# Transposing the normed x tiles by DMA, SBUF to SBUF, in place of TensorE transposes

## The chip, the cores and the metric

The kernel runs on the 8 cores of one Trainium2 chip. Each core computes 2048 of the 16384 tokens, with no traffic between cores. The metric is the device time of the slowest core in microseconds (us).

## The reference

One decoder block on x of shape (2, 8192, 2048), float32. Two gated token mixers share one input projection:

```python
h = rmsnorm(x, norm1_g[l])
proj = h @ w_in[l]                    # (B, T, 15872)
# mixer A: dilated windows (128,1), (512,4), (2048,16), 3 groups of 8 heads, merged by denominators
# mixer B: window 128, 16 query heads over 2 kv heads, with sinks
merged = gate_a * (o_a @ w_branch_a[l]) + gate_b * (o_b @ w_branch_b[l])
x = x + merged @ w_out[l]
h2 = rmsnorm(x, norm2_g[l])
x = x + jnp.square(jax.nn.relu(h2 @ w_ff1[l])) @ w_ff2[l]
```

## The kernel before

A core holds its own 2048 tokens and the 2048 before them (the halo, needed by the window of 2048): 4096 rows of x, loaded as 32 tiles of 128 rows x 2048 columns float32. The first stage norms each tile and turns it round, so that the 2048 features lie on the partitions, in 16 chunks of 128: hH holds the halo, hO the own tokens, both as [128, 16, 2048] bf16. The rest of the kernel multiplies weights with these two: keys and values of mixer A and B, then queries with the attention, the gates, the output projection and the MLP.

The instructions of each engine are written out in order by helpers (P.op, P.group, P.dma); each carries the waits that its buffers ask for. Five queues run side by side: PE, ACT, DVE, POOL (loads weights) and SP (all other DMAs of this stage). An instruction that waits holds up all behind it on its own queue.

The stage that the change touches is a loop over j = 0 to 31 that begins each turn with norm_tile(j + 2) and transpose_tile(j + 1), and then multiplies: va_job(1, j - 4) from j = 4 on and va_job(0, j) always. A va_job is 16 matmuls of tile j against 512 columns of w_in (L395), an eviction by ACT (L403) or DVE (L406) to vst, and a store of 128 KB by SP (L413). After the loop four va_jobs of slab 1 are left, then the key heads of the 2048 window start (L494).

norm_tile(j) does, on ACT, the sum of squares of the loaded tile xt (L363, its elementwise result is thrown away into xs), then a logarithm and an exponential (L365, L367) for the scale; on DVE the multiplication by scale and gain into xs (L369), bf16; then SP is asked for the load of tile j + 3 (xload, L351), 1 MB. There are three xt and two xs. transpose_tile(j) does 16 TensorE transposes in two groups of 8 into PSUM banks 4 to 7 (L380), which ACT (L388) and DVE (L390) copy to hH or hO, 1024 elements a partition each.

The whole order of a turn:

```python
    for j in range(32):
        if j + 2 < 32:
            norm_tile(j + 2)
        if j + 1 < 32:
            transpose_tile(j + 1)
        if j >= LEAD:
            va_job(1, j - LEAD)
        va_job(0, j)
```

From the 41st va_job on, tick() has POOL copy a piece of the MLP weights to DRAM as bf16 at every fourth job (w1c, L323).

Of the kernel before, what the change touches and what calls it, by code (L numbers as in the profile page):

```python
# [11 lines left out]
BF16 = mybir.dt.bfloat16  # L12
AF = mybir.ActivationFunctionType
# [4 lines left out]
TOWN = 2048  # L18
# [224 lines left out]
def build_program():  # L243
    nc = bass.Bass("TRN2", target_bir_lowering=False)

    def dram(name, shape, dt, kind):
        return nc.dram_tensor(name, list(shape), dt, kind=kind).ap()
# [14 lines left out]
    out = dram("out", [NCH, 128, TOWN], F32, "ExternalOutput")  # L262
# [10 lines left out]
    P = Prog(nc)  # L273
    psum = [nc.alloc_psum_tensor(f"bank{i}", [128, 512], F32) for i in range(8)]
    bank = [Buf(f"bank{i}") for i in range(8)]
# [3 lines left out]
    ident = carea.at("ident", [128, 128], BF16, 0)  # L279
# [6 lines left out]
    st = [carea.at(f"st{i}", [128, 4], F32, 768 + 32 * i) for i in range(3)]  # L286
# [10 lines left out]
    B_const = Buf("consts")  # L297
# [30 lines left out]
    hO = A.at("hO", [128, NCH, TOWN], BF16, OWN)  # L328
    hH = A.at("hH", [128, NCH, TOWN], BF16, HAL)
    B_h = [Buf(f"h{j}") for j in range(32)]  # L330
# [9 lines left out]
    xt = [A.at(f"xt{i}", [128, D], F32, RX + 8192 * i) for i in range(3)]  # L340
    B_xt = [Buf(f"xt{i}") for i in range(3)]
    xs = [A.at(f"xs{i}", [128, D], BF16, RX + 24576 + 4096 * i) for i in range(2)]
    B_xs = [Buf(f"xs{i}") for i in range(2)]
    B_st = [Buf(f"st{i}") for i in range(3)]
    vst = [A.at(f"vst{i}", [128, 512], BF16, VST + 1024 * i) for i in range(4)]
    B_vst = [Buf(f"vst{i}") for i in range(4)]
    B_vn = {g: Buf("vn_" + g) for g in vn}
# [2 lines left out]
    def xload(j):  # L350
        P.dma("sp", lambda e: e.dma_start(out=xt[j % 3][:], in_=xe[128 * j:128 * j + 128, :]), B_xt[j % 3],  # L351
              writes=[B_xt[j % 3]])
# [7 lines left out]

    def norm_tile(j):
        s, x3, t3 = j % 2, j % 3, j % 3
        P.op("act", lambda e: e.activation(out=xs[s][:], in_=xt[x3][:], func=AF.Square, accum_out=st[t3][:, 0:1]),  # L363
             reads=[B_xt[x3]], writes=[B_xs[s], B_st[t3]])
        P.op("act", lambda e: e.activation(out=st[t3][:, 1:2], in_=st[t3][:, 0:1], func=AF.Ln, scale=1.0 / D,  # L365
                                           bias=EPS), writes=[B_st[t3]])
        P.op("act", lambda e: e.activation(out=st[t3][:, 2:3], in_=st[t3][:, 1:2], func=AF.Exp, scale=-0.5),  # L367
             writes=[B_st[t3]])
        P.op("dve", lambda e: e.scalar_tensor_tensor(out=xs[s][:], in0=xt[x3][:], scalar=st[t3][:, 2:3], in1=g1b[:],  # L369
                                                     op0=ALU.mult, op1=ALU.mult),  # L370
             reads=[B_xt[x3], B_st[t3], B_g1b], writes=[B_xs[s]])
        if j + 3 < 32:
            xload(j + 3)

    def transpose_tile(j):
        s = j % 2
        for half in range(2):
            bi = 4 + (2 * j + half) % 4
            pb = psum[bi][:].bitcast(BF16)
            fns = [(lambda e, c=8 * half + k, k=k, pb=pb, s=s: e.transpose(  # L380
                out=pb[:, 128 * k:128 * k + 128], in_=xs[s][:, 128 * c:128 * c + 128], identity=ident[:]))
                for k in range(8)]
            P.group("pe", fns, reads=[B_xs[s], B_const], writes=[bank[bi]])
            h, t0 = (hH, 128 * j) if j < 16 else (hO, 128 * j - TOWN)
            dst = h[:, 8 * half:8 * half + 8, t0:t0 + 128]
            src = pb.rearrange("p (a b) -> p a b", a=8)
            if half == 0:
                P.op("act", lambda e, dst=dst, src=src: e.copy(out=dst, in_=src), reads=[bank[bi]], adds=[B_h[j]])  # L388
            else:
                P.op("dve", lambda e, dst=dst, src=src: e.tensor_copy(out=dst, in_=src), reads=[bank[bi]],  # L390
                     adds=[B_h[j]])

    def v_block(lhs, bufs, wps, kper, ncols, g, blk, col0, bi):

# [40 lines left out]

    LEAD = 4
    norm_tile(0)
    P.dma("sp", lambda e: e.dma_start(out=gvec[:], in_=gvec_in[:, :]), cb2, writes=[cb2])
    P.dma("sp", lambda e: e.dma_start(out=esink[:], in_=sinks_in.partition_broadcast(128)), cb3, writes=[cb3])
    P.dma("sp", lambda e: e.dma_start(out=g2[:], in_=g2_in[:, :]), cb4, writes=[cb4])  # L440
    P.dma("sp", lambda e: e.dma_start(out=rtab[:], in_=rtab_in[:, :, :]), B_rtab, writes=[B_rtab])
    norm_tile(1)
    transpose_tile(0)
# [8 lines that stand above are left out]
# [33 lines left out]
    def main_bank():  # L485
        bi = mctr[0] % mode["main"]
        mctr[0] += 1
        return bi
# [336 lines left out]
    for st_ in range(STEPS):  # L825
        u, f = divmod(st_, 4)
# [29 lines left out]
    for i in range(24):  # L856
        P.dma("sp", lambda e, i=i: e.dma_start(out=oT[:, i, :], in_=oTd[i]), B_oT[i], reads=[B_oTd[i]],  # L857
              writes=[B_oT[i]])
# [33 lines left out]
    for i, (n, tb) in enumerate(its):  # L892
        if i + 2 < len(its):
# [5 lines left out]
        fns = [(lambda e, k=k, tsl=tsl, b1=b1, wa=wa: e.matmul(psum[b1][:, :], lhsT=wa[:, 128 * k:128 * k + 128],  # L899
                                                              rhs=oT[:, k, tsl], start=(k == 0), stop=(k == 7)))  # L900
               for k in range(8)]
        P.group("pe", fns, reads=[ba] + B_oT[:8], writes=[bank[b1]])
        fns = [(lambda e, k=k, tsl=tsl, b2=b2, wbt=wbt: e.matmul(  # L903
            psum[b2][:, :], lhsT=wbt[:, 128 * k:128 * k + 128], rhs=oT[:, 8 + k, tsl], start=(k == 0),
            stop=(k == 15))) for k in range(16)]
# [4 lines left out]
        s = 2 * (i % 3)  # L910
        for j, b in ((0, b1), (1, b2)):
# [4 lines left out]
             reads=[B_gt[s], B_gt[s + 1]], adds=[B_mT[n]])  # L916
# [45 lines left out]
    for i, (n, tb) in enumerate(its):  # L962
        wt, wb = ld.get(pc[0] + n)
        if i + NXT - 1 < len(its):
            xrload(i + NXT - 1)
        bi = main_bank()
        fns = [(lambda e, k=k, tb=tb, bi=bi, wt=wt: e.matmul(  # L967
            psum[bi][:, :], lhsT=wt[:, 128 * k:128 * k + 128], rhs=mT[:, k, 512 * tb:512 * tb + 512],
            start=(k == 0), stop=(k == NCH - 1))) for k in range(NCH)]
# [51 lines left out]
    for tb in range(4):  # L1021
        tsl = slice(512 * tb, 512 * tb + 512)
        for sl in range(16):
# [3 lines left out]
            for ci in range(4):  # L1027
                j = 4 * sl + ci
                bi = main_bank()
                fns = [(lambda e, k=k, ci=ci, bi=bi, wt=wt, tsl=tsl: e.matmul(  # L1030
                    psum[bi][:, :], lhsT=wt[:, 512 * k + 128 * ci:512 * k + 128 * ci + 128],
                    rhs=h2T[:, k, tsl], start=(k == 0), stop=(k == NCH - 1))) for k in range(NCH)]
# [4 lines left out]
                     reads=[bank[bi]], writes=[B_rt[rs_]])  # L1037
                P.op("dve", lambda e, bi=bi, rs_=rs_, j=j: e.scalar_tensor_tensor(  # L1038
                    out=uT[:, j, :], in0=psum[bi][:, :], scalar=0.0, in1=rt[rs_][:], op0=ALU.max, op1=ALU.mult),
                    reads=[bank[bi], B_rt[rs_]], writes=[B_u[j]])  # L1040
# [4 lines left out]
        for n in range(NCH):  # L1045
# [6 lines left out]
                  reads=[B_x2s], writes=[B_yr[ys]])  # L1052
            bi = main_bank()
            for j0 in range(0, 64, 16):
                fns = [(lambda e, j=j, bi=bi, wt=wt: e.matmul(  # L1055
                    psum[bi][:, :], lhsT=wt[:, 128 * j:128 * j + 128], rhs=uT[:, j, :],
                    start=(j == 0), stop=(j == 63))) for j in range(j0, j0 + 16)]
                P.group("pe", fns, reads=[wb] + B_u[j0:j0 + 16], writes=[bank[bi]])
            P.op("dve", lambda e, bi=bi, yos=yos, tsl=tsl: e.tensor_tensor(  # L1059
                out=yo[yos][:], in0=psum[bi][:, :], in1=r2b[:, tsl], op=ALU.mult),  # L1060
                reads=[bank[bi], B_r2[tb]], writes=[B_yo[yos]])
            P.op("dve", lambda e, yos=yos, ys=ys: e.tensor_tensor(out=yo[yos][:], in0=yo[yos][:], in1=yr[ys][:],
                                                                 op=ALU.add),
                 reads=[B_yr[ys]], writes=[B_yo[yos]])
            P.dma("sp", lambda e, yos=yos, n=n, tsl=tsl: e.dma_start(out=out[n, :, tsl], in_=yo[yos][:]), B_yo[yos],
                  reads=[B_yo[yos]])
# [114 lines left out]
```

How the kernel before makes its waits and increments, by code:

```python
    def replay(self, eng_name, eng):  # L141
        waited = {}
        for waits, fn, s, n in self.q[eng_name]:
            for ws, v in waits:
                if waited.get(ws.name, 0) < v:
                    eng.wait_ge(ws.h, v)
                    waited[ws.name] = v
            if fn is None:
                continue
            ins = fn(eng)
            if s is not None:
                ins.then_inc(s.h, n)
```

## Time and profile before

| | us |
|---|---|
| three runs | 4761.35, 4761.61, 5371.22; median 4761.61 |
| the profiled execution | 4764.82 |
| its slowest core, from first to last instruction (core 5) | 4763.3 |
| the other seven cores | 4723.3 to 4758.1 |
| PE busy | 4663.0 (98%) |
| first stage, up to the first key matmul (L494) | 296.5 |

The profile is of core 5. Its times count from the first instruction. A "busy" PE has matmuls under way; they are pipelined, so the mean of a single one (379 ns for 512 columns) is longer than what one adds to a stream (16 in 3.45 us). A releaser is what ended the idle time of an engine.

### The profile page before, as it was taken

The numbers are of one execution on the slowest core, as the hardware profiler recorded it, in microseconds if no ns is written. First come the engines' busy times: TensorE is split into PE (matmuls) and PEld (weight loads), VectorE is DVE, ScalarE is ACT, GpSimd is POOL, SyncE is SP. The second block draws the span as 40 slices with busy tenths as digits, with TensorE's granted clock in tenths as the row PEclk, the third lists the DMA queues.
The fourth block names the chain that finished last, engine by engine and source line by source line (L and its number), as shares of the span: only waits on it lengthen the run. The fifth ranks groups of instructions, "written<-read, shape, count | busy, mean of one in ns | idle before, by whom it ended". The sixth has DMA issues, their size and how long they took to land.

```text
span 4763.3 us, 64896 instructions; the slowest of 8 cores (4723.3 to 4763.3 us)
## 1 busy us (share of the span) xinstructions
PE 4663.0 (98%) x24018; PEld 2228.6 (47%) x24018; DVE 1607.2 (34%) x1806; ACT 1394.1 (29%) x2424; POOL 294.9 (6%) x560
## 2 busy tenths in 40 slices
PE   6999999988999999999999999999999999999999
PEld 3544445544455455555444444444444444444444
DVE  3446650112555555655424433210121111101111
ACT  4534430034455555555412233210011001001100
POOL 0000000000011111111110000000000000000000
PEclk9999999999999999999999999999999999999999
DMA  8685567775666556565486666435534544454354
GB/s 203 173 132 91 104 98 106 128 118 95 125 113 131 118 132 137 110 138 110 106 211 137 145 178 180 166 145 191 192 144 168 185 177 159 162 196 168 146 190 144
DMA packets 225766, 696.94 MB, mean 146 GB/s; under 512 B 96944, under 2 KB 109232, under 8 KB 200752
## 3 DMA queue, kind: packets, MB, share of 16 engines
q0 software_dynamic: 57536, 455.12, 39.8%
q1 hardware_dynamic: 167920, 237.67, 17.1%
q8 instruction: 197, 3.23, 0.3%
q14 instruction: 113, 0.93, 0.1%
HBM read 727.70 MB, written 185.20 MB: 192 GB/s over the span
## 4 chain that ended last, share of the span: by engine, by line
PE 94%; DMA 3%; ACT 1%; SPq 1%; issue 0%; DVE 0%; DVEq 0%; ACTq 0%
PE bank L494 22%; PE bank L1030 19%; PE bank L1055 19%; PE bank L395 10%; PE bank L804 7%; PE bank L967 5%; PE bank L903 5%; PE bank L899 2%; PE bank L749 1%; PE bank L509 1%; PE bank L700 1%; PE bank L754 1%; DMA oTd<-ost 1%; DMA xt<-xe 1%; SPq L857 1%; DMA vn_a<-vst 1%
## 5 line engine op out<-in xcount | busy, mean ns | idle before, releaser
L494 PE MATMUL bank<-hO,w 128*128 128x512 bf16 x3968 | 915.9, 381 | 12.8 <-DVE Qt L519 12.8
L1030 PE MATMUL bank<-h2T,ws 128*128 128x512 bf16 x4096 | 886.0, 379 | 2.1 <-ACT h2T L950 2.1
L1055 PE MATMUL bank<-uT,ws 128*128 128x512 bf16 x4096 | 884.7, 379 | 0.0
L1030 PEld LDWEIGHTS bank<-h2T,ws 128*128 128x128 bf16 x4096 | 401.1, 98 | 486.7 <-issue 4.7
L1055 PEld LDWEIGHTS bank<-uT,ws 128*128 128x128 bf16 x4096 | 400.8, 98 | 483.3
L494 PEld LDWEIGHTS bank<-hO,w 128*128 128x128 bf16 x3968 | 382.4, 98 | 446.2 <-issue 23.6
L1036 ACT ACTIVATE rt<-bank 128x512 f32<-128x512 f32 x256 | 152.8, 597 | 1394.2 <-PE bank L1030 1394.2
L804 PE MATMUL bank<-hO,w 128*128 128x512 bf16 x2048 | 476.6, 379 | 0.0
L1038 DVE SCALAR_TENSOR_TENSOR uT<-bank,rt 128x512 bf16<-128x512 f32 x256 | 177.1, 692 | 711.2 <-ACT rt L1036 711.2
L519 DVE SCALAR_TENSOR_TENSOR kst<-bank,gvec,rb 128x512 bf16<-128x512 f32 (+1 forms) x154 | 293.3, 1904 | 254.7 <-ACT rb L513 249.2
L395 PE MATMUL bank<-w,hO 128*128 128x512 bf16 (+1 forms) x1472 | 304.1, 363 | 10.7 <-DVE vst L406 10.7
L804 PEld LDWEIGHTS bank<-hO,w 128*128 128x128 bf16 x2048 | 200.3, 98 | 241.2
L1059 DVE TENSOR_TENSOR yo<-bank,r2b 128x512 f32<-128x512 f32 x64 | 44.3, 692 | 788.7 <-PE bank L1055 788.7
L502 ACT ACTIVATE sq<-bank 128x512 bf16<-128x512 f32 x314 | 183.9, 586 | 413.7 <-PE bank L494 413.7
L519 DVE SCALAR_TENSOR_TENSOR Qt<-bank,gvs,rb 128x512 bf16<-128x512 f32 x160 | 232.0, 1450 | 162.5 <-ACT rb L513 162.4
L511 ACT ACTIVATE rb<-bank 128x512 f32<-128x512 f32 x314 | 183.8, 585 | 251.3 <-PE bank L509 249.4
L903 PE MATMUL bank<-oT,w 128*128 128x512 bf16 x1024 | 233.3, 381 | 3.7 <-DMA oT<-oTd 3.7
L967 PE MATMUL bank<-mT,w 128*128 128x512 bf16 x1024 | 221.3, 379 | 0.1
L395 PEld LDWEIGHTS bank<-w,hO 128*128 128x128 bf16 x1472 | 150.6, 103 | 150.0 <-issue 10.9
L513 ACT ACTIVATE rb<-rb 128x512 f32<-128x512 f32 x314 | 194.5, 620 | 29.0 <-ACT rb L511 0.4
L704 ACT ACTIVATE Pexp<-bank 128x512 f32<-128x512 f32 x320 | 173.4, 596 | 54.7 <-PE bank L700 53.9
L406 DVE CAST vst<-bank 128x512 bf16<-128x512 f32 (+1 forms) x77 | 51.0, 664 | 407.5 <-PE bank L395 334.2
(100 smaller groups left out, 3443.9 us busy)
## 6 DMA issues: line engine op xcount, KB each, us to landing
ws<-w1c POOLq DMA_DIRECT2D x64, 2048.0 KB, 8.2
ws<-w2c POOLq DMA_DIRECT2D x64, 2048.0 KB, 8.9
w<-w_in POOLq DMA_DIRECT2D x115, 512.0 KB, 8.1
xt<-xe SPq DMA_DIRECT2D x32, 1024.0 KB, 6.3
w1c<-w_ff POOLq DMA_DIRECT2D x64, 512.0 KB, 7.5
w2c<-w_ff POOLq DMA_DIRECT2D x64, 512.0 KB, 7.1
gz<-zst POOLq DMA_DIRECT2D x128, 256.0 KB, 3.7
gt<-gz SPq DMA_DIRECT2D x128, 256.0 KB, 4.3
```

The source lines that it names most:

```text
L395: fns = [(lambda e, k=k: e.matmul(psum[bi][:, 0:ncols], lhsT=lhs[k], rhs=wps[k // kper][0][:, (k % kper) * ncols:(k % kper + 1) * ncols], ...
L494: fns = [(lambda e, k=k: e.matmul(psum[bi][:, 0:n], lhsT=wt[:, 128 * k:128 * k + 128], rhs=hB[:, k, :] if last else hsl(k, t0, n), start=( ...
L502: P.op("act", lambda e: e.activation(out=sq[es][:, 0:n], in_=psum[bi][:, 0:n], func=AF.Square), reads=[bank[bi]], writes=[B_sq[es]])
L511: P.op("act", lambda e: e.activation(out=rb[er][:, 0:n], in_=psum[b2][:, 0:n], func=AF.Ln, bias=128.0 * EPS), reads=[bank[b2]], writes=[B_ ...
L513: P.op("act", lambda e: e.activation(out=rb[er][:, 0:n], in_=rb[er][:, 0:n], func=AF.Exp, scale=-0.5), writes=[B_rb[er]])
L519: P.op("dve", lambda e: e.scalar_tensor_tensor(out=dst, in0=src, scalar=gsrc[:, gcol:gcol + 1], in1=r, op0=ALU.mult, op1=ALU.mult), reads= ...
L804: fns = [(lambda e, k=k: e.matmul(psum[bi][:, :], lhsT=wt[:, 128 * k:128 * k + 128], rhs=hO[:, k, 512 * tb:512 * tb + 512], start=(k == 0) ...
L903: fns = [(lambda e, k=k, tsl=tsl, b2=b2, wbt=wbt: e.matmul(psum[b2][:, :], lhsT=wbt[:, 128 * k:128 * k + 128], rhs=oT[:, 8 + k, tsl], star ...
L967: fns = [(lambda e, k=k, tb=tb, bi=bi, wt=wt: e.matmul(psum[bi][:, :], lhsT=wt[:, 128 * k:128 * k + 128], rhs=mT[:, k, 512 * tb:512 * tb + ...
L1030: fns = [(lambda e, k=k, ci=ci, bi=bi, wt=wt, tsl=tsl: e.matmul(psum[bi][:, :], lhsT=wt[:, 512 * k + 128 * ci:512 * k + 128 * ci + 128], r ...
L1038: P.op("dve", lambda e, bi=bi, rs_=rs_, j=j: e.scalar_tensor_tensor(out=uT[:, j, :], in0=psum[bi][:, :], scalar=0.0, in1=rt[rs_][:], op0=A ...
L1055: fns = [(lambda e, j=j, bi=bi, wt=wt: e.matmul(psum[bi][:, :], lhsT=wt[:, 128 * j:128 * j + 128], rhs=uT[:, j, :], start=(j == 0), stop=( ...
```

## The change

transpose_tile no longer uses TensorE. SP issues one DMA transpose for each tile, from xs straight into the tile's 128 columns of hH or hO. Each of the two xs has a semaphore of its own for it (B_tr). The 512 transposes on PE, the 32 copies on ACT and the 32 on DVE are gone. The sum of squares now throws its elementwise result into hH or hO, where the transpose overwrites it, no longer into xs.

```diff
--- before.py
+++ after.py
@@ -342,6 +342,7 @@
     xs = [A.at(f"xs{i}", [128, D], BF16, RX + 24576 + 4096 * i) for i in range(2)]
     B_xs = [Buf(f"xs{i}") for i in range(2)]
     B_st = [Buf(f"st{i}") for i in range(3)]
+    B_tr = [Buf(f"tr{i}") for i in range(2)]
     vst = [A.at(f"vst{i}", [128, 512], BF16, VST + 1024 * i) for i in range(4)]
     B_vst = [Buf(f"vst{i}") for i in range(4)]
     B_vn = {g: Buf("vn_" + g) for g in vn}
@@ -360,8 +361,10 @@
 
     def norm_tile(j):
         s, x3, t3 = j % 2, j % 3, j % 3
-        P.op("act", lambda e: e.activation(out=xs[s][:], in_=xt[x3][:], func=AF.Square, accum_out=st[t3][:, 0:1]),
-             reads=[B_xt[x3]], writes=[B_xs[s], B_st[t3]])
+        h, t0 = (hH, 128 * j) if j < 16 else (hO, 128 * j - TOWN)
+        P.op("act", lambda e: e.activation(out=h[:, :, t0:t0 + 128], in_=xt[x3][:].rearrange("p (a b) -> p a b", a=16),
+                                           func=AF.Square, accum_out=st[t3][:, 0:1]),
+             reads=[B_xt[x3]], writes=[B_h[j], B_st[t3]])
         P.op("act", lambda e: e.activation(out=st[t3][:, 1:2], in_=st[t3][:, 0:1], func=AF.Ln, scale=1.0 / D,
                                            bias=EPS), writes=[B_st[t3]])
         P.op("act", lambda e: e.activation(out=st[t3][:, 2:3], in_=st[t3][:, 1:2], func=AF.Exp, scale=-0.5),
@@ -374,21 +377,9 @@
 
     def transpose_tile(j):
         s = j % 2
-        for half in range(2):
-            bi = 4 + (2 * j + half) % 4
-            pb = psum[bi][:].bitcast(BF16)
-            fns = [(lambda e, c=8 * half + k, k=k, pb=pb, s=s: e.transpose(
-                out=pb[:, 128 * k:128 * k + 128], in_=xs[s][:, 128 * c:128 * c + 128], identity=ident[:]))
-                for k in range(8)]
-            P.group("pe", fns, reads=[B_xs[s], B_const], writes=[bank[bi]])
-            h, t0 = (hH, 128 * j) if j < 16 else (hO, 128 * j - TOWN)
-            dst = h[:, 8 * half:8 * half + 8, t0:t0 + 128]
-            src = pb.rearrange("p (a b) -> p a b", a=8)
-            if half == 0:
-                P.op("act", lambda e, dst=dst, src=src: e.copy(out=dst, in_=src), reads=[bank[bi]], adds=[B_h[j]])
-            else:
-                P.op("dve", lambda e, dst=dst, src=src: e.tensor_copy(out=dst, in_=src), reads=[bank[bi]],
-                     adds=[B_h[j]])
+        h, t0 = (hH, 128 * j) if j < 16 else (hO, 128 * j - TOWN)
+        P.dma("sp", lambda e: e.dma_start_transpose(out=h[:, :, t0:t0 + 128], in_=xs[s][:]), B_tr[s],
+              reads=[B_xs[s]], writes=[B_h[j]])
 
     def v_block(lhs, bufs, wps, kper, ncols, g, blk, col0, bi):
```

The SP queue, where tile 6 is transposed and the tiles 10 and 11 are loaded (xt1 and xt2; hH is the halo's h, vn_a2 the value store of the 2048 window). Before:

```order
L413 DMA vn_a2<-vst1_19_71 128x4x128 [waits prog_dve]
L351 DMA xt1_14_66<-xe 128x2048 [waits d_xt1,prog_act,prog_dve]
L413 DMA vn_a2<-vst2_20_72 128x4x128 [waits prog_act]
L413 DMA vn_a2<-vst3_21_73 128x4x128 [waits prog_dve]
L351 DMA xt2_15_67<-xe 128x2048 [waits d_xt2,prog_act,prog_dve]
L413 DMA vn_a2<-vst0_18_70 128x4x128 [waits prog_act]
L413 DMA vn_a2<-vst1_19_71 128x4x128 [waits prog_dve]
```

After:

```order
L404 DMA vn_a2<-vst1_19_71 128x4x128 [waits prog_dve]
L352 DMA xt1_14_66<-xe 128x2048 [waits d_xt1,prog_act,prog_dve]
L381 DMA_TRANSPOSE hH_11_63<-xs0_16_68 128x16x128
L404 DMA vn_a2<-vst2_20_72 128x4x128 [waits prog_act]
L404 DMA vn_a2<-vst3_21_73 128x4x128 [waits prog_dve]
L352 DMA xt2_15_67<-xe 128x2048 [waits d_xt2,prog_act,prog_dve]
L381 DMA_TRANSPOSE hH_11_63<-xs1_17_69 128x16x128
L404 DMA vn_a2<-vst0_18_70 128x4x128 [waits prog_act]
```

Each transpose stands right behind a load of 1 MB. That load waits for a later step of DVE than the transpose needs, so the transpose has no wait of its own left. Behind it stand the two value stores.

The DVE queue around the norms of tiles 6 and 7 (waits are by semaphore: d_xt1 is the load of xt1, d_tr0 the transpose that reads xs0). Before:

```order
L406 CAST vst3_21_73<-bank3 128x512 [waits prog_pe]
L369 SCALAR_TENSOR_TENSOR xs0_16_68<-xt0_13_65,st0_8_50,g1b_12_64 128x2048 [waits d_xt0,prog_act]
L390 COPY hH_11_63<-bank7 128x8x128 [waits prog_pe]
L406 CAST vst1_19_71<-bank1 128x512 [waits prog_pe,prog_dve,d_vst1]
L369 SCALAR_TENSOR_TENSOR xs1_17_69<-xt1_14_66,st1_9_51,g1b_12_64 128x2048 [waits d_xt1,prog_act]
L390 COPY hH_11_63<-bank5 128x8x128 [waits prog_pe]
L406 CAST vst3_21_73<-bank3 128x512 [waits prog_pe,prog_dve,d_vst3]
```

After:

```order
L397 CAST vst3_21_73<-bank3 128x512 [waits prog_pe]
L372 SCALAR_TENSOR_TENSOR xs0_16_68<-xt0_13_65,st0_8_50,g1b_12_64 128x2048 [waits d_xt0,prog_act,prog_dve,d_tr0]
L397 CAST vst1_19_71<-bank1 128x512 [waits prog_pe,d_vst1]
L372 SCALAR_TENSOR_TENSOR xs1_17_69<-xt1_14_66,st1_9_51,g1b_12_64 128x2048 [waits d_xt1,prog_act,prog_dve,d_tr1]
L397 CAST vst3_21_73<-bank3 128x512 [waits prog_pe,prog_dve,d_vst3]
```

The copies out of PSUM are gone, and each norm multiplication waits for the transpose of the tile two ahead of it, which read the same xs.

The PE queue from the end of va_job(0, 4) over va_job(1, 1) to the start of va_job(0, 5), with slab 1 in w4 to w7 and slab 0 in w0 to w3. Before:

```order
L395 MATMUL bank1<-w2_4_56,hH_11_63 128x512 x4
L395 MATMUL bank1<-w3_5_57,hH_11_63 128x512 x4
L380 MATMUL bank4<-ident_1_43,xs0_16_68 128x128 [waits prog_dve]
L380 MATMUL bank4<-ident_1_43,xs0_16_68 128x128 x7
L380 MATMUL bank5<-ident_1_43,xs0_16_68 128x128 x8
L395 MATMUL bank2<-w4_6_58,hH_11_63 128x512 x4
L395 MATMUL bank2<-w5_7_59,hH_11_63 128x512 x4
L395 MATMUL bank2<-w6_8_60,hH_11_63 128x512 x4
L395 MATMUL bank2<-w7_9_61,hH_11_63 128x512 x4
L395 MATMUL bank3<-w0_2_54,hH_11_63 128x512 [waits prog_act,prog_dve]
L395 MATMUL bank3<-w0_2_54,hH_11_63 128x512 x3
```

After:

```order
L386 MATMUL bank1<-w3_5_57,hH_11_63 128x512 x4
L386 MATMUL bank2<-w4_6_58,hH_11_63 128x512 [waits prog_act]
L386 MATMUL bank2<-w4_6_58,hH_11_63 128x512 x3
L386 MATMUL bank2<-w5_7_59,hH_11_63 128x512 x4
L386 MATMUL bank2<-w6_8_60,hH_11_63 128x512 x4
L386 MATMUL bank2<-w7_9_61,hH_11_63 128x512 x4
L386 MATMUL bank3<-w0_2_54,hH_11_63 128x512 [waits d_tr1,prog_dve]
```

The 16 transposes between two pairs of jobs are gone, and the slab 0 job of each tile waits for that tile's DMA transpose (d_tr1), where it had waited for the two copies.

## Rows read from the trace of the kernel before

**Rows 1.** The page: its head, the engines, the chain by line.

```profile
span 4763.3 us, 64896 instructions; the slowest of 8 cores (4723.3 to 4763.3 us)
...
PE 4663.0 (98%) x24018; PEld 2228.6 (47%) x24018; DVE 1607.2 (34%) x1806; ACT 1394.1 (29%) x2424; POOL 294.9 (6%) x560
...
PE bank L494 22%; PE bank L1030 19%; PE bank L1055 19%; PE bank L395 10%; PE bank L804 7%; PE bank L967 5%; PE bank L903 5%; PE bank L899 2%; PE bank L749 1%; PE bank L509 1%; PE bank L700 1%; PE bank L754 1%; DMA oTd<-ost 1%; DMA xt<-xe 1%; SPq L857 1%; DMA vn_a<-vst 1%
```

**Rows 2.** The chain in order of time, 0 to 340 us: start, length, what.

```profile
27.69 25.28 DMA xt<-xe
...
58.36 1.87 PE bank L380 x16
60.22 5.11 PE bank L395 x16
...
88.73 0.89 PE bank L380 x16
89.62 6.91 PE bank L395 x32
...
269.02 27.63 PE bank L395 x128
296.65 4.75 PE bank L494 x22
```

**Rows 3.** Stretches of the stage: busy time by engine, clock, DMA share, GB/s.

```profile
core 5: us, PE busy (x) PEld busy (x) DVE busy (x) ACT busy (x) POOL busy (x), PEclk, DMA share, GB/s
...
40.00:58.00 18.00, 5.27 (x36) 2.54 (x34) 5.38 (x4) 5.13 (x8) 0.00 (x0) 0.77 0.99 232
...
82.00:230.00 148.00, 148.00 (x913) 76.36 (x911) 67.27 (x58) 73.96 (x115) 1.00 (x2) 1.00 0.65 172
```

**Rows 4.** Groups by line, 80 to 240 us: busy, mean ns, idle before.

```profile
L369 DVE SCALAR_TENSOR_TENSOR xs<-xt,st,g1b 128x2048 bf16<-128x2048 f32 x21 | 49.2, 2342 | 0.0
...
L380 PE MATMUL bank<-ident,xs 128*128 128x128 bf16 x336 | 22.2, 219 | 0.0
...
L388 ACT COPY hO<-bank 128x1024 bf16<-128x1024 bf16 x12 | 12.1, 1012 | 9.2 <-PE bank L380 9.2
```

**Rows 5.** The timeline around one steady tile, 81 to 93 us.

```profile
81.17 0.69 DVE L406 CAST vst<-bank 128x512 bf16<-128x512 f32 x1 [4.25 <-PE bank L395]
81.78 2.34 DVE L369 SCALAR_TENSOR_TENSOR xs<-xt,st,g1b 128x2048 bf16<-128x2048 f32 x1
...
84.20 0.35 SPq L351 DMA_DIRECT2D xt<-xe  x1
86.08 4.02 SPq L413 DMA_DIRECT2D vn_a<-vst  x2
```

**Rows 6.** DMAs issued from 84.19 to 84.3 us.

```profile
xt<-xe SPq DMA_DIRECT2D x1, 1024.0 KB, 5.7
```

**Rows 7.** DMAs issued from 86.0 to 86.2 us.

```profile
vn_a<-vst SPq DMA_DIRECT2D x1, 128.0 KB, 4.3
```

**Rows 8.** DMA from 81.9 to 84.2 us, one store: 40 slices of 0.0575 us.

```profile
GB/s 36 45 62 36 45 36 36 178 36 27 18 18 9 0 0 22 102 196 223 236 227 200 223 223 200 209 121 80 18 0 0 0 0 0 0 0 0 0 0 0
...
q1 hardware_dynamic: 633, 0.16, 28.5%
...
vn_a<-vst SPq DMA_DIRECT2D x1, 128.0 KB, 2.1
```

**Rows 9.** Line L351, the loads of x, 80 to 235 us.

```profile
DMA to landing us min/median/max: 5.7/6.1/12.0
```

**Rows 10.** POOL's timeline: the weight copies that begin in this stage.

```profile
210.61 0.51 POOL L323 DMA_DIRECT2D w1c<-w_ff  x1 [178.65 <-PE bank L395]
226.20 0.49 POOL L323 DMA_DIRECT2D w1c<-w_ff  x1 [15.08 <-PE bank L395]
...
280.80 0.56 POOL L202 DMA_DIRECT2D w<-w_in  x1 [7.32 <-PE bank L395]
```

**Rows 11.** DMAs issued from 230 to 235 us, beside such a copy.

```profile
xt<-xe SPq DMA_DIRECT2D x1, 1024.0 KB, 9.8
```

## The prediction

> **What bounds the kernel now.** I read the page first: PE is busy for 4663.0 of 4763.3 us and almost the whole chain is matmuls [rows 1]. A change of the first stage can then pay only by what it takes off PE there, and can cost all that it makes PE wait. Next the chain in order of time [rows 2]. Up to 58.36 us the stage waits for loads of x: one of them takes 25.28 us to land, with the DMA engines at 0.99 of their time and PE busy for 5.27 of 18 us [rows 3]. From 58.36 to 296.65 us PE runs without a gap: each tile takes 0.89 us of transposes and 6.91 us of matmuls (two va_jobs of 3.455), 7.80 in all. In the steady stretch PE is full, DVE and ACT are busy for less than half, and the DMA engines for 0.65 [rows 3]. So DMA has some room on average. The question is what stands one behind the other.
>
> **What is removed.** 32 tiles x 0.89 us = 28.5 us of PE. Those of tiles 0 to 3, ahead of 58.36 us, lie in a stretch that waits for loads; the other 28 x 0.89 = 25 us, plus 1.0 because those at 58.36 ran slowly (1.87), can be won: 26 us, 0.5% of the kernel. The copies on ACT (1.01 us a tile) and DVE (0.68) lie beside PE's work and are worth nothing by themselves [rows 4]. The sum of squares has the same number of elements with another destination: nothing, as ACT is half idle. Removing these takes nothing off the later stages either, which do not see the first one except by its end.
>
> **What is added, and the loop that it closes.** In the queue listings of the change, the norm multiplication of tile j+2 waits until the DMA transpose of tile j has landed, since there are two xs. SP's load of tile j+5 waits for that multiplication, and the transpose of j+1 stands right behind this load. The multiplication of j+3 waits for that transpose. So the transposes no longer overlap: one period holds, in a row,
> (a) from landing to DVE's start, 0.15 us (an estimate, from the 0.1 to 0.2 us between dependent steps in the timeline);
> (b) the multiplication, 2.34 us [rows 5];
> (c) its start at 81.78 to the load's issue at 84.20 is 2.42, so 0.1 more [rows 5];
> (d) the load, 1 MB: 5.7 us from issue to landing here, 6.1 in the median [rows 6, 9];
> (e) the transpose's own 512 KB, D.
> That (e) comes after (d) and not beside it is what rows 5 to 7 show: a store issued at 86.08, behind the load of 84.20 on the same queue, landed 4.3 us later, at 90.4, half a microsecond after the load (89.9). A store with nothing ahead of it lands in 2.1 us [rows 8]. The transposes go by the same SP queue.
>
> **The price D.** No DMA transpose is in this trace. The nearest row is the store: 256-byte packets, like a 128-column piece of an xs row. While it flows the slices read about 200 to 236 GB/s, so 524,288 bytes take about 2.4 us [rows 8]; by the half microsecond that 128 KB came after the load it is 4 x 0.5 = 2.0. From below: if the transpose ran entirely beside the load, D = 0. From above: the same store costs 0.285 x 16 x 2.3 us / 633 = 16.6 ns of an engine for each packet. Were the turned-round data written in pieces of 16 elements, 16,384 of them, it would be 16,384 x 16.6 ns / 16 = 17 us. I take 2.4, the row with the like packet size and count per byte. SP's time to issue it is unknown as well (a load takes 0.35); up to about 5 us it is hidden, since the load ahead of it is still draining.
>
> The Trainium skill, Advanced Engine Details and Errata, section X-Bar Transpose (TRN2), says that transposing DMAs are as fast as regular ones, at 350 to 400 GB/s. By that D would be an estimated 1.4 us, the period 1.0 shorter, and the sum 27 us less, at the 2% line. No row here reaches this rate for small packets, so I stay with 2.4.
>
> **The sum.** Period P = 0.15 + 2.34 + 0.1 + 6.1 + 2.4 = 11.1 us, against PE's 6.91 a tile: PE waits about 4 us in each.
> Start: the transpose of tile 0 is issued at about 28 us, behind the load that lands at 27.69 + 25.28 = 53.0 [rows 2], and lands at 53.0 + 2.4, say 55.4. No later norm can go before it.
> Loads stand ahead of the transposes of tiles 1 to 27 (the last load is of tile 31), so tile 27 lands at 55.4 + 27 x 11.1 = 355. Weight copies begin at the 41st va_job and then every fourth, that is every second tile, three of them on this part [rows 10]. Beside such a copy a load took 9.8 us instead of 6.1, up to 12.0 [rows 9, 11]; 3 x 4 = 12 us more, which gives 367. From there PE is fed: the last four transposes have no load ahead and land in some 4 us each (2.4 of data and 1.3 of the lone store's 2.1 that is not its data, about 0.8), under PE's 6.91. What PE still has to do is 13 va_jobs (five of slab 0, eight of slab 1), 13 x 3.455 = 45 us. The stage ends at 412 instead of 296.65: 115 us more.
> Whether PE's clock falls in the waits changes this little: after a gap PE's first 16 matmuls took 5.11 us instead of 3.45 [rows 2], which makes 8.6 us of work in a period of 11.1, and still fits.
> All later stages are as before. ACT, DVE and the stores have their room: the eviction of a tile's slab 0 job comes about 4.3 us after the landing, well within the period. The profiled execution of 4764.8 becomes 4880; against the median of the runs, 3 us lower, 4877. I say 4878.
>
> **Rivals.**
> 1. *The transposes run beside the loads (not slower).* If SP's engines served a transpose while the load ahead still streams, it would land in about 2.4 + 1.3 us, and the period would be 0.15 + 2.34 + 0.1 + 0.35 (issue of the load) + 3.7 = 6.6, less than PE's 6.91. PE then does 64 va_jobs x 3.455 = 221 us from 55.4 on, and the stage ends near 278, 18 us early: 4745. With the start of before it would be 4735. It decides below P of about 7. For it speaks the idle third of the DMA time [rows 3]; against it the store that landed behind the load [rows 6, 7]. From P = 10.3 down the result is within 2% (27 x 0.8 us less than the sum). Chance of the parallel case 0.17.
> 2. *A dear transpose.* At D = 17 the loaded periods are 25.7 and the last four about 19: 55 + 15 + 27 x 25.7 + 4 x 19 + 12 = 852, then five va_jobs, 17 us: 869, or 5335 us. It stands on nothing but unknown packet and issue costs. The Trainium skill, VectorE: DVE Perf Modes, section The three transpose paths, gives 1309 ns for a 128x128 transpose by DMA against 390 on TensorE; 16 in a row would be an estimated 21 us, P near 30 and the total near 5450. No row here shows it. Chance 0.12, for the mechanism and this rule together.
> 3. *In between,* D of 4 to 10 us because SP issues the pieces slower than the load drains, or the weight copies hurt more: P of 12.7 to 18, so 27 x 1.6 to 27 x 7 more, 4920 to 5065. Chance 0.18.
> 4. *The change as forecast,* P of 10.1 to 12.6: 4850 to 4920. Chance 0.53.
> That the PE transposes and copies are really gone is in the queue listings.
>
> **How the numbers follow.** About 2% (95 us, 4857) is what a measurement of this kernel can tell from no change. Faster by 2% would need 95 us and the stage has 26 to give: 0.01. Within 2%: rival 1 (0.17) and the lowest part of the forecast, with D near 1.5 (0.10): 0.27. Slower: 0.72. For the range I leave out rival 2 alone and reach down to rival 1: 4735 to 5065.
>
> **What the profile after would show.** PE without L380 and idle before the va_job line, its idle time put down to the DMA transpose, about 4 us a tile; DVE's multiplication waiting for the transpose of two tiles ahead; the loads of x issued every 11 us instead of 7.8; a transpose that lands 8 to 9 us after its issue while loads stand ahead of it, and in some 4 us in the last four tiles; the first key matmul at about 412 us; later stages of equal length. The forecast is wrong if the landing time in the last four tiles is far from 4 us (D mis-sized), if transposes with a load ahead land as fast as those without (rival 1), if SP's issue of one takes more than 5 us (rivals 2 and 3), or if the first tile lands far from 55 us.

## The result, and the profile after

| | before | changed |
|---|---|---|
| runs, us | 4761.35 to 4767.72 | 4858.46, 4858.61, 4864.77, 4866.66; median 4861.69 |
| ratio, 95% interval | 1 | 1.0205 [1.0191, 1.022] |
| profiled execution, us | 4764.82 | 4866.66 |
| its slowest core, us | 4763.3 (core 5) | 4865.1 (core 4) |
| first key matmul on that core, us | 296.5 | 398.5 |

The change makes the kernel about 98 us slower, 2.05%. The interval excludes no change by far, but it reaches from 1.91% to 2.2%, so it does not say whether the loss is above or below 2%. Cores of a die are in some executions held at a lower clock, whatever the kernel; such runs are left out here and below.

The page of the changed kernel: the head, the engines, the chain by line, and the value matmuls (L386, which was L395).

```profile
span 4865.1 us, 63344 instructions; the slowest of 8 cores (4824.4 to 4865.1 us)
...
PE 4637.9 (95%) x23045; PEld 2203.3 (45%) x23506; DVE 1590.6 (33%) x1774; ACT 1362.4 (28%) x2392; POOL 295.7 (6%) x560
...
PE 88%; DMA 7%; DVE 2%; SPq 1%; issue 1%; ACT 1%; DVEq 0%; ACTq 0%
...
L386 PE MATMUL bank<-w,hO 128*128 128x512 bf16 (+1 forms) x1446 | 314.0, 373 | 47.9 <-DMA hO<-xs 36.5
...
L386 PE MATMUL bank<-w,hH 128*128 128x512 bf16 x597 | 152.7, 415 | 107.1 <-DMA hH<-xs 106.0
```

The chain by engine of the kernel before:

```profile
PE 94%; DMA 3%; ACT 1%; SPq 1%; issue 0%; DVE 0%; DVEq 0%; ACTq 0%
```

The transposes of PE are gone, and PE now stands idle for 155 us ahead of the value matmuls, 142 of it ended by a DMA transpose. DMA's part of the chain has gone from 3% to 7%, DVE's from 0 to 2%. All that is added lies in the first stage: behind the first key matmul both slowest cores need 4466.6 to 4466.8 us (4763.3 - 296.5 and 4865.1 - 398.5).

The chain of the changed kernel in order of time, of 0 to 440 us: start, length, what. It answers to [rows 2].

```profile
28.54 31.77 DMA hH<-xs
60.40 2.36 DVE xs L372
...
156.63 2.36 DVE xs L372
159.05 0.35 SPq L352
159.45 7.89 DMA hH<-xs
167.43 2.36 DVE xs L372
169.86 0.34 SPq L352
170.25 7.54 DMA hH<-xs
...
342.04 9.15 DMA hO<-xs
351.19 0.24 issue
351.44 9.46 PE bank L386 x33
...
398.67 4.75 PE bank L485 x22
```

From 60.4 to 351.2 us the chain never touches PE. Multiplication, issue of the load, transpose, multiplication again: the loop that the prediction drew, 10.8 us in this turn. The timeline has the multiplications start at 60.40 and, 22 turns later, at 293.61: 10.6 us a turn. The last five turns, beside the weight copies, take 11.5 each.

How long a transpose takes from issue to landing, for those that write hH; SP's issue of it; then the landing of those that write hO; and SP's timeline at the end of the stage.

```profile
L381 SPq DMA_TRANSPOSE hH<-xs x16: 5097/5460/27537, 28.5 to 212.0; - x16
...
DMA to landing us min/median/max: 6.6/7.6/31.8
...
DMA to landing us min/median/max: 4.3/7.6/9.2
```

```profile
342.04 7.60 SPq L381 DMA_TRANSPOSE hO<-xs  x1
349.74 1.08 SPq L404 DMA_DIRECT2D vn_a<-vst  x2
350.87 1.57 SPq L381 DMA_TRANSPOSE hO<-xs  x1
```

With a load ahead a transpose lands after 7.6 us. The last four have none ahead, but stores and a weight copy beside them, and land after 5.4, 4.6, 6.8 and 4.3. SP needs 1.6 to 1.9 us to issue three of these four (the other took 4.0) and over 5 when a load is ahead, so what the queue shows there is mostly the wait for the load, not a price of the transpose. The page counts 292,321 DMA packets instead of 225,766, which is 2080 a transpose, and 16.78 MB more, which is the 524,288 bytes of each: 2048 packets of 256 bytes and 32 that add next to nothing.

### The profile page after: what moved, and what is told of

Its sections match the earlier page's. It is cut to its first block, busy times and chain, and to the rows that moved or that the text cites. A ratio compares the mean times of both kernels' runs of the same rounds, so it can differ in the third digit from the quotient of the medians.

```text
span 4865.1 us, 63344 instructions; the slowest of 8 cores (4824.4 to 4865.1 us)
## 1 busy us (share of the span) xinstructions
PE 4637.9 (95%) x23045; PEld 2203.3 (45%) x23506; DVE 1590.6 (33%) x1774; ACT 1362.4 (28%) x2392; POOL 295.7 (6%) x560
## 2 busy tenths in 40 slices
DMA packets 292321, 713.65 MB, mean 147 GB/s; under 512 B 163504, under 2 KB 175792, under 8 KB 267312
## 4 chain that ended last, share of the span: by engine, by line
PE 88%; DMA 7%; DVE 2%; SPq 1%; issue 1%; ACT 1%; DVEq 0%; ACTq 0%
PE bank L485 21%; PE bank L1021 18%; PE bank L1046 18%; PE bank L795 7%; PE bank L386 6%; PE bank L958 5%; PE bank L894 5%; DMA hH<-xs 3%; PE bank L890 2%; DMA hO<-xs 2%; PE bank L740 1%; PE bank L691 1%; PE bank L500 1%; DVE xs L372 1%; PE bank L745 1%
## 5 line engine op out<-in xcount | busy, mean ns | idle before, releaser
L485 PE MATMUL bank<-hO,w 128*128 128x512 bf16 x3839 | 895.7, 380 | 15.5 <-DVE Qt L510 9.4
L795 PE MATMUL bank<-hO,w 128*128 128x512 bf16 x2004 | 474.7, 379 | 2.5 <-issue 0.2
L386 PE MATMUL bank<-w,hO 128*128 128x512 bf16 (+1 forms) x1446 | 314.0, 373 | 47.9 <-DMA hO<-xs 36.5
L386 PE MATMUL bank<-w,hH 128*128 128x512 bf16 x597 | 152.7, 415 | 107.1 <-DMA hH<-xs 106.0
L386 PEld LDWEIGHTS bank<-w,hO 128*128 128x128 bf16 x1472 | 153.3, 105 | 200.6 <-issue 69.1
L394 ACT CAST vst<-bank 128x512 bf16<-128x512 f32 (+1 forms) x78 | 43.8, 562 | 544.7 <-PE bank L386 501.5
## 6 DMA issues: line engine op xcount, KB each, us to landing
ws<-w2c POOLq DMA_DIRECT2D x64, 2048.0 KB, 11.1
```

What stands on the lines that cost most here:

```text
L386: fns = [(lambda e, k=k: e.matmul(psum[bi][:, 0:ncols], lhsT=lhs[k], rhs=wps[k // kper][0][:, (k % kper) * ncols:(k % kper + 1) * ncols], ...
L485: fns = [(lambda e, k=k: e.matmul(psum[bi][:, 0:n], lhsT=wt[:, 128 * k:128 * k + 128], rhs=hB[:, k, :] if last else hsl(k, t0, n), start=( ...
L795: fns = [(lambda e, k=k: e.matmul(psum[bi][:, :], lhsT=wt[:, 128 * k:128 * k + 128], rhs=hO[:, k, 512 * tb:512 * tb + 512], start=(k == 0) ...
```

## The experiments

Ratios are to the kernel before on the same chip; the chips differ by up to about 6 us, so two kernels from different chips are compared by their ratios. Ratios without an interval rest on one or two runs. "Turn" is the distance between two norm multiplications in the steady stretch (for the kernel before, PE's), "landing" the median from issue to landing there, "end" the first key matmul, median of the 8 cores of the profiled execution.

| kernel | us, ratio | turn | landing | end |
|---|---|---|---|---|
| before | 4762, 1 | 7.80 | | 295.8 |
| changed | 4862, 1.0205 | 10.6 | 7.6 | 396.9 |
| transpose ahead of its turn's load | 4771, 1.0035 [1.0021, 1.005] | 7.25 | 7.6 | 317.6 |
| the same, loop closed again | 4783, 1.0058 [1.004, 1.0076] | 7.5 | 4.9 | 326.9 |
| transposes from ACT's queue | 4884 and 4887, 1.027 | 11.5 | 7.9 | 432.6 |
| loads from ACT's queue | 4774, 1.003 | 7.4 | 7.0 to 7.9 | 314.4 |
| two transposes a tile | 4909, 1.032 | 12.9 | | 455.4 |
| no loads after the third | 4745, 0.998 | 6.9 | 4.4 | 285.9 |
| tiles 0 to 3 by TensorE | 4827, 1.0147 [1.0125, 1.0169] | 10.5 | 7.4 | 369.8 |
| every second tile from 9 on by DMA (12 of 32), the rest by TensorE | 4745, 0.9970 [0.9958, 0.9981] | 7.35 | 4.9 to 5.4 | 285.4 |
| tiles 0 to 7 by TensorE, rest ahead of the load | 4749, 0.9984 [0.9972, 0.9995] | 6.9, then 7.2 | 7.0 to 8.7 | 295.1 |
| tiles 0 to 7 by TensorE, loop closed | 4757, 1.0001 [0.9989, 1.0012] | 7.6 | 4.8 | 300.8 |

Theory A: the transposes wait for one another through the load that stands between them, because it is ahead on the same queue. Theory B: a DMA transpose is slow by itself. Theory C: as A, but it is the DMA engines that load and transpose share, not the queue.

**The load moved behind the transpose.** Out of norm_tile, and into the loop over the tiles:

```diff
-        if j + 3 < 32:
-            xload(j + 3)
...
         if j + 2 < 32:
             norm_tile(j + 2)
         if j + 1 < 32:
             transpose_tile(j + 1)
+        if j + 5 < 32:
+            xload(j + 5)
```

The load of tile 3 stands behind norm_tile(0) as before, that of tile 4 behind norm_tile(1) and the transpose of tile 0.

> The changed kernel with one thing moved: in each turn the transpose of tile j+1 is issued ahead of the load of tile j+5, not behind it. Same instructions, same two xs. Theory A (the period of 10.5 us comes from the loop in which each transpose stands behind a load of 1 MB that waits for the previous transpose): the loop is cut, the period falls to what PE (6.91 us) or the DMA engines (0.69 of 10.5 = 7.2 us busy a tile) allow, about 7.5 us, the first key matmul comes at 300 to 320 us and the kernel at 4765 to 4790 us. Theory B (the 7.6 us from issue to landing are the transpose's own): period and time stay, 10.5 us and about 4862 us.

Measured: 4771 us, ratio 1.0035, as A and C have it. B is out: with the same 32 transposes and the same bytes, some 80% of the loss is gone (83% by the ratio, 78% by the stage's end). The landing stayed at 7.6 us, but two transposes are now under way at once, and the DMA engines have no idle time left. Stretches of this kernel: busy time of PE, PEld, DVE, ACT, POOL, clock, DMA share, GB/s.

```profile
82.00:230.00 148.00, 138.72 (x634) 61.15 (x633) 59.42 (x40) 57.84 (x100) 0.51 (x1) 0.99 1.08 248
```

The turn of 7.25 us is shorter than a landing, so the loop no longer bounds it. The share of DMA is 1.08 beside 0.65 before [rows 3]; that DMA is the new bound is read from this row.

**The transposes on a queue of their own.**

```diff
-        P.dma("sp", lambda e: e.dma_start_transpose(out=h[:, :, t0:t0 + 128], in_=xs[s][:]), B_tr[s],
-              reads=[B_xs[s]], writes=[B_h[j]])
+        P.dma("act", lambda e: e.dma_start_transpose(out=h[:, :, t0:t0 + 128], in_=xs[s][:]), B_tr[s],
+              reads=[B_xs[s], B_xs[1 - s]], writes=[B_h[j]])
```

> The changed kernel with the transposes issued from ACT's queue instead of SP's, and made to wait, as before, for the norm multiplication of tile j+2, so that load and transpose still start together but stand on different queues. Theory A (a transpose waits because the load is ahead of it on the same queue): it lands 4.3 to 6 us after its issue, the period is 7 to 8.7 us, the kernel 4770 to 4815 us. Rival C (the queue does not matter, load and transpose share the DMA engines and both end after about 7.5 us): landing 7 to 8 us, period 10 to 10.5, kernel within 10 us of 4862.

A falls, C stands. ACT's timeline and SP's show both issues at 153.30 us, and the DMA queues by stretch (q1 is SP's, q10 ACT's: packets, MB, share) show who was served, from 155.3 to 156.3, from 157.3 to 158.3 and from 159.3 to 160.3 us.

```profile
153.30 0.35 SPq L352 DMA_DIRECT2D xt<-xe  x1
153.30 5.67 ACTq L381 DMA_TRANSPOSE hH<-xs  x1
```

```profile
q1 hardware_dynamic: 31, 0.25, 84.6%
...
q1 hardware_dynamic: 49, 0.34, 82.4%
q10 hardware_dynamic: 92, 0.02, 10.3%
...
q10 hardware_dynamic: 1129, 0.28, 125.9%
```

The load's 8 KB packets go first, and those of the transpose, although on another queue and issued in the same instant, begin some four microseconds after that. The landing is 7.9 us, beside 7.6 on SP's queue. The turn of 11.5 us and the ratio of 1.027 are above what C expected. They have a cause of their own, seen in the chain: the issue holds ACT for 5.67 us, behind it stand an eviction and the sum of squares, and the next multiplication at 162.44 waits for these, not for the transpose.

**The loads on ACT's queue.**

```diff
-        P.dma("sp", lambda e: e.dma_start(out=xt[j % 3][:], in_=xe[128 * j:128 * j + 128, :]), B_xt[j % 3],
+        P.dma("sp" if j < 3 else "act", lambda e: e.dma_start(out=xt[j % 3][:], in_=xe[128 * j:128 * j + 128, :]), B_xt[j % 3],
```

> The changed kernel with the loads of x from tile 3 on issued from ACT's queue, transposes left on SP's, and the order of both otherwise kept, so that a load and the transpose behind it start together on two queues. If a transpose landed late only because the load was ahead of it on its queue (theory A), it lands 4.3 to 5.5 us after its issue in the steady stretch, with periods of 7 to 8.5 us. If the DMA engines are what both share and large packets get most of them (theory C, which the run with transposes on ACT's queue speaks for), it lands after 7 to 8 us as before and the period stays at 10 to 11 us.

The expectation overlooked half of the edit. With the load off SP's queue the transpose no longer stands behind its wait for the multiplication, so the loop is open as in the first experiment: ratio 1.003 beside 1.0035. The landing, 7.0 to 7.9 us, is C's, not A's. So this run tells again that opening the loop gives the time back, and nothing new on the queues.

**The loop closed again, with the load behind.** On top of the first edit:

```diff
-              reads=[B_xs[s]], writes=[B_h[j]])
+              reads=[B_xs[s], B_xs[1 - s]], writes=[B_h[j]])
```

> The run with each transpose ahead of the load of the same turn, with the wait for the norm multiplication of tile j+2 put back by hand, so that the loop of two xs is closed again exactly as in the changed kernel and only the place of the load differs: behind the transpose, not ahead of it. If the load ahead is what makes the loop long (theory C: 1 MB goes through the DMA engines first, then the 512 KB), a transpose now finds at most the end of the load of the turn before, lands after 4.4 to 6 us, and the period is 2.6 + 4.4 to 6 = 7.0 to 8.6 us; kernel 1.002 to 1.01 of the kernel before. If the closed loop itself costs, whatever stands ahead (rival W), the period is near 10 us and the kernel at 1.017 to 1.02.

The chain of this kernel:

```profile
157.09 2.36 DVE xs L372
159.52 4.68 DMA hH<-xs
164.29 2.36 DVE xs L372
166.71 4.93 DMA hH<-xs
171.74 2.36 DVE xs L372
```

The landing falls to 4.9 us in the median and the turn to 7.5, with the wait in place. Rival W is out: the closed loop is cheap, and the megabyte between two of its steps is what costs 3 us a turn.

**The price of a transpose: two of them, and none of the loads.**

```diff
+    B_tr2 = [Buf(f"trb{i}") for i in range(2)]
...
         P.dma("sp", lambda e: e.dma_start_transpose(out=h[:, :, t0:t0 + 128], in_=xs[s][:]), B_tr[s],
               reads=[B_xs[s]], writes=[B_h[j]])
+        if j + 8 < 32:
+            k = j + 8
+            h2, t2 = (hH, 128 * k) if k < 16 else (hO, 128 * k - TOWN)
+            P.dma("sp", lambda e: e.dma_start_transpose(out=h2[:, :, t2:t2 + 128], in_=xs[s][:]), B_tr2[s],
+                  reads=[B_xs[s]], writes=[B_h[k]])
```

> The changed kernel with a second DMA transpose of the same xs right behind the first for tiles 0 to 23, into the place of tile j+8, which is overwritten later: extra work only, to measure the price of one transpose in the loop. If it costs its data, 512 KB at the rate of the 256-byte packets, each doubled period is 2.0 to 2.4 us longer and the kernel about 4865 + 24 x 2.2 = 4918 us. If it costs a full lone landing (4.3 us) or its issue and landing one after the other, 4 to 6 us a period, 4960 to 5010 us.

Its multiplications start at 74.76 and, ten turns later, at 203.29: 12.85 us a turn. Those of the changed kernel, at 83.07 and 209.20 with twelve turns between, take 10.51. A transpose more in the loop costs 2.34 us, which is 224 GB/s; over the stage 455.4 - 396.9 = 58.5 us for 24 of them, 2.44 each. The ratios, 1.032 and 1.0205, are 57 us apart.

The loads after the third left out:

```diff
-        if j + 3 < 32:
-            xload(j + 3)
```

> The changed kernel with only the first three tiles of x loaded and used again for all others (the output is not that of the reference). The transposes and all waits on them stay. Theory A: with no load ahead a transpose lands in about 4.3 us, the loop takes 2.6 + 4.3 = 6.9 us and PE is fed nearly without a gap; with the earlier start the first key matmul comes at 260 to 275 us and the kernel at about 4725 to 4740 us. Theory B (landing 7.6 us by itself): period 10 us or more, 4840 us or more.

The landing of 4.4 us and the turn are as expected, and B is out once more. The turn of 6.91 us is PE's own work for a tile (49 matmuls take 10.74 us here, which makes 7.0 for 32), so it is only a ceiling for the loop. The end at 286 us instead of 260 to 275 is not as expected: the first transpose, issued at 18.2 with only the three first tiles loaded, still lands at 61.8. The chain and, from 41 to 51 us, the DMA queues (q0 is POOL's, with the weights):

```profile
18.20 43.61 DMA hH<-xs
61.80 0.14 issue
61.94 5.78 PE bank L384 x16
```

```profile
q0 software_dynamic: 118, 0.45, 82.0%
q1 hardware_dynamic: 337, 0.09, 48.2%
```

In ten microseconds 0.09 MB of the transpose moved beside 0.45 of weights. By an estimate from these shares a packet on SP's queue took 0.482 x 16 x 10 us / 337 = 229 ns beside the weights; in the third stretch of the run with transposes on ACT's queue, with nothing beside them, it was 1.259 x 16 x 1 us / 1129 = 18 ns.

**The start given back.** Tiles 0 to 3 as before the change, in norm_tile and transpose_tile:

```diff
+        if j < 4:
+            for half in range(2):
...
+            return
         P.dma("sp", lambda e: e.dma_start_transpose(out=h[:, :, t0:t0 + 128], in_=xs[s][:]), B_tr[s],
```

> The changed kernel with tiles 0 to 3 transposed by TensorE as before the change, and tiles 4 to 31 by DMA. It gives back the start alone: tile 0's transpose was issued at 28.5 us and landed at 60.3, and nothing later could begin. Expected: four tiles are multiplied before 60 us as before the change, the loop of 10.6 us runs 23 times from about 66 us, the first key matmul comes at about 362 us instead of 398.7, and the kernel takes about 4826 us. If the start were not on the path (the loop from tile 4 on would in any case begin only when the loads are there), the gain is under 10 us.

The kernel time is as expected, 4827 us; the stage's end is 27 us earlier instead of 37. The loop takes 10.5 us a turn as before, but tile 4 lands at 70.6 instead of 66, and the six turns beside the weight copies take 12.5 each. The start is worth about as much in the kernels below: 22 us between the first experiment (317.6) and its version with tiles 0 to 7 on TensorE (295.1), 26 with the loop closed (326.9 and 300.8).

**Versions that might win.** In all, the first tiles stay with TensorE, and a DMA transpose stands ahead of the load of its turn. In the first the condition for TensorE is j < 8 or j % 2 == 0, in the second and third j < 8; the third has the loop closed as above, the first two issue right behind the tile's own norm. Shown for the first; the second has j >= 8 alone:

```diff
+        if j >= 8 and j % 2:
+            transpose_tile(j)
         if j + 3 < 32:
             xload(j + 3)
```

> Half of the transposes by each: tiles 0 to 7 and all even tiles by TensorE as before the change, the odd tiles from 9 on by DMA, each issued right behind its norm and ahead of the next load. PE's turn falls from 7.80 to 7.36 us on the mean, the DMA engines' from 7.2 to about 6.2 us a tile, so neither is full. Expected: 12 x 0.89 = 11 us less than the kernel before, about 4747 us beside 4758, ratio 0.998. If DMA transposes are delayed beyond two turns by the loads, PE waits appear and it is no faster than before.

> Tiles 0 to 7 by TensorE as before the change, all later ones by DMA, issued right behind their norm and ahead of the next load (no loop through a load). PE's turn is 6.91 us, the DMA engines have 7.2 us of work a tile and set the pace if they reach full use. Expected: periods of 7.3 to 7.8 us, 24 x (0 to 0.5) less than before, 4746 to 4760 us, ratio 0.997 to 1.0. If the DMA engines are delayed further (weight copies, HBM), the period is above 7.8 and it is slower than before by up to 15 us, as the run with transposes ahead of the loads, whose period was 7.8.

> As the run before, with tiles 0 to 7 transposed by TensorE as before the change: the start is given back and the transposes take turns with the loads. If the turns come down to PE's or the DMA engines' 6.9 to 7.3 us, the stage ends 12 to 20 us before 296.5 us and the ratio is 0.996 to 0.998, as good as the half and half version (0.997). If each turn stays at 7.8 us or more, 1.0 or above.

The first, with 12 tiles on DMA, is the fastest kernel of the study: 4745 us, ratio 0.9970, 13 us or 0.3% under the kernel before, as expected. The second gains about half of that, inside its range. The third gains nothing: its turn came down to 7.6 us and not to the 6.9 to 7.3 that a gain needed, and the stage ends 5 us later than before. Stretches of the first and then of the second:

```profile
82.00:230.00 148.00, 147.21 (x791) 72.02 (x805) 64.94 (x51) 66.14 (x108) 1.00 (x2) 1.00 0.93 205
```

```profile
82.00:230.00 148.00, 139.91 (x631) 63.00 (x642) 59.25 (x41) 57.45 (x98) 1.00 (x2) 0.98 1.05 235
```

With every tile from 8 on by DMA its share is 1.05 and PE waits 8 us of the 148; with every second one it is 0.93 and PE waits for less than 1. But a share of 1 is not by itself what stops PE. The second version once more, cut at 200 us, with PE's two long waits and two of the weight copies that POOL issues:

```profile
82.00:200.00 118.00, 117.42 (x538) 53.52 (x547) 50.12 (x35) 48.48 (x82) 0.51 (x1) 1.00 1.07 240
200.00:260.00 60.00, 41.87 (x174) 17.77 (x177) 17.57 (x11) 15.72 (x31) 1.47 (x3) 0.86 1.03 204
```

```profile
195.21 0.51 POOL L323 DMA_DIRECT2D w1c<-w_ff  x1 [164.34 <-PE bank L409]
208.34 15.82 PE L409 MATMUL bank<-w,hO 128*128 128x512 bf16 x62 [6.76 <-DMA hO<-xs]
232.39 0.49 POOL L323 DMA_DIRECT2D w1c<-w_ff  x1 [14.12 <-PE bank L409]
249.30 15.82 PE L409 MATMUL bank<-w,hO 128*128 128x512 bf16 x63 [10.51 <-DMA hO<-xs]
```

Up to 200 us, at a share of 1.07, PE is fed: its turns are 6.91 us up to 150 and 7.2 behind that, and it waits 0.6 us of 118. It waits 18 us of the next 60, in the part of the stage with the weight copies, and that is most of the 24 x 0.89 = 21 us that DMA took off it. The transposes issued from 150 to 194 us land after 7.5 us in the median, those from 194 to 230 after 9.9. That the copies cause this is not shown, since no run leaves them out. This profiled execution took 4757 us, 8 more than the median of its kernel, so the waits are likely shorter in others.

**The changed kernel again,** unaltered, on the chip of the two closed-loop runs.

> The changed kernel itself, unaltered, on the same chip as the runs of this group and beside the kernel before, so that their differences can be read without the difference between chips. Expected: ratio 1.0205, period 10.4 to 10.8 us, first key matmul at 395 to 400 us.

4850.5 and 4852.1 us beside 4754 to 4762 of the kernel before there, a ratio of about 1.020, turn 10.5 us, landing 7.5 us, end 396.6: the measured loss is not one chip's.

## Why the prediction was right, step by step

The forecast was 4878 us and slower; 4861.7 was measured. The mechanism, a loop through two xs with a load in it, is the one that the runs show. That the number is as near as 16 us is in part luck: the terms below err by 7.5 us one way and by 20.5 the other. The range, 4735 to 5065, was wide enough to hold a faster kernel too. The prediction took 2% for what can be told from no change; the interval above is 0.15% on either side, so this loss is told easily; whether it is above 2% is not. Its terms:

- **What can be won, 26 us.** 12 of the 32 tiles taken off PE gave 10.4 us of the stage, and 12 x 0.89 is 10.7, so the price of 0.89 us a tile holds where DMA has room. In the changed kernel none of it shows.
- **The loop through two xs.** Right, and shown by undoing it in two ways: the load moved (7.25 us a turn) and the loop kept but with the load behind (7.5).
- **That the load is ahead of the transpose.** Right in size, too narrow in its reason. The prediction read from [rows 5 to 7] that a store waits behind a load on the same queue. The run with the transposes on ACT's queue shows that another queue does not help.
- **D, 2.4 us.** The doubled transposes give 2.34 to 2.44. The bounds of 0 and 17 us were far off; the store's row, with its 256-byte packets, was the right neighbour. By the Trainium skill's Advanced Engine Details and Errata, X-Bar Transpose (TRN2), at 350 to 400 GB/s, D would be an estimated 1.4 us; the 2.34 us here are 224 GB/s, and the measurement decides.
- **The period, 11.1 us against 10.6.** (d) and (e) were 6.1 + 2.4 = 8.5 us from the load's issue; in the steady turns it is 0.4 + 7.6 = 8.0. The load still took its 6 us (5.9 in the median from 83 to 209 us), and the transpose landed 2 us behind it, less than the 2.34 that a second one adds: its first packets flow before the load's last, as the stretch from 157.3 us of the run with transposes on ACT's queue shows. Over 27 turns this is 13.5 us too much.
- **The weight copies, 12 us.** 5 x (11.53 - 10.6) = 5 us in this profile, 7 too much. In the run with tiles 0 to 3 on TensorE six turns beside the copies cost 12 us more than steady ones, and in the second run of the changed kernel 14, so this term differs from run to run.
- **The first landing, 55.4 us.** It was 60.3: 5 too little. The load ahead landed at 54.8, and the transpose 5.5 us behind it instead of 2.4. I had not counted the weights on POOL's queue. That they held it up fits the run without loads, where a packet took 229 ns beside them, but no run has the loads and not the weights.
- **The tail, 45 us for 13 va_jobs.** 47.5, since PE begins it slowly: the first 33 matmuls take 9.46 us. The last four transposes were expected to land in some 4 us each and took 4.3 to 6.8, which PE's work in hand hid.
- **PE's clock.** In 82 to 230 us the granted clock was 0.89 on the mean, 1.00 before the change [rows 3]. After a wait of 0.76 us PE did 32 matmuls in 7.07 us; after one of 3.33 us the next 31 took 8.75 (from 156.78 to 165.53):

```profile
146.39 7.07 PE L386 MATMUL bank<-w,hH 128*128 128x512 bf16 x32 [0.76 <-DMA hH<-xs]
156.78 2.94 PE L386 MATMUL bank<-w,hH 128*128 128x512 bf16 x9 [3.33 <-DMA hH<-xs]
159.94 5.59 PE L386 MATMUL bank<-w,hH 128*128 128x512 bf16 x22 [0.22 <-issue]
```

The stretches of these two bursts, with the clock in the third column from the end:

```profile
146.40:153.40 7.00, 7.00 (x32) 3.02 (x32) 2.88 (x2) 2.27 (x4) 0.00 (x0) 1.00 0.52 154
156.80:165.50 8.70, 8.48 (x31) 3.44 (x32) 2.87 (x2) 0.00 (x0) 0.00 (x0) 0.80 0.56 148
```

The first burst had 2.4 GHz (1.00), the second 0.80 of it on the mean, so a part of it ran at 1.2 GHz. That costs 1.7 us and, as forecast (8.6 us of work), it fits into the loop's 10.6.
- **The rivals.** That transposes run beside the loads needed landings near 3.7 us; there are none under 4.3. The dear transpose is out by D; so is the estimate of 21 us from the Trainium skill's VectorE: DVE Perf Modes, The three transpose paths, since sixteen blocks in one transfer cost 2.34 us and not sixteen times the 1.309 of one. The third rival's slow issue is out too: without a load ahead SP issues one in 1.6 to 1.9 us. The prediction named an issue over 5 us as a sign against itself; the issues did take 5.1 to 7.6 (the first 27.5), but that time is mostly the load's, which the prediction had itself allowed for. In the first experiment the change as it might have been written, the transpose ahead of the load, is 0.35% slower than before: the place of the load in SP's queue was worth about 80 us (1.0205 and 1.0035; the stage ends 79 us apart).

With these terms as the same profile shows them the sum gives 412 + 5 - 13.5 - 7 + 2.5 = 399, and 398.7 was measured: no term is left out. The rest of the kernel was left alone, as said.

## What to carry to other kernels

When work moves from a full engine to DMA, follow the buffer's chain from landing to landing and list all that is queued in it: here 2.4 us of new work made a turn of 10.6, because 1 MB of somebody else's stood between. Put the transfer that the chain waits for ahead of the prefetch, and count DMA's own share afterwards: with every tile from 8 on moved it was full, which PE did not feel until the part of the stage with the weight copies, and 12 tiles of 32 was the best that was tried.

## What the runs showed that I had not expected

- Two transfers issued in the same instant on two queues were not served side by side: the one with 8 KB packets moved 0.25 MB in the microsecond in which the one with 256-byte packets had not begun. The issue, too, held ACT's queue for 5.67 us, though no load stood there. Whether the size of the packets decides, or the kind of the transfer, was not tried.
- The first transpose took 31.8 us, and 43.6 without the later loads of x, while weights came in on POOL's queue; with no load ahead it takes 4.3 at the least.
- Behind the first key matmul the eight cores of one execution need between 4429.1 and 4466.8 us with the kernel before. The slowest core's time alone is therefore a rough measure of one stage, and the table has the stage's end as the median of the eight cores.
